# Gate columns moved to the prompt stage, batched state-space tables, and a third PSUM bank for turned weights in an NSA + S5 hybrid decoder step

## The reference

```
proj = einsum('ntd,de->nte', h, w_in)                      # h: normalised, modulated rows
o_cmp = attention over compressed keys (one per 16 tokens, window 32)
o_slc = attention over the 16 best blocks of 64 keys
o_win = attention over the last 512 keys
g_nsa = sigmoid(g_nsa)                                      # one gate for each branch, head and token
o     = g_nsa[0]*o_cmp + g_nsa[1]*o_slc + g_nsa[2]*o_win
# S5: h_t = a*h_{t-1} + B u_t (complex, 32 groups of 64 states, 16 inputs), y = Re(C h) + d*u
o_ssm = gelu(y) * sigmoid(gelu(y) @ w_glu)
x = x + mod2 * ((sigmoid(g_a)*(o @ w_br_attn) + sigmoid(g_s)*(o_ssm @ w_br_ssm)) @ w_out)
y = rms_norm(x + mod5 * (relu(norm(x) @ w_ff1)**2 @ w_ff2), g_final)
```

## Time and profile before

| what | value |
|---|---|
| three runs | 2451.07, 2453.78, 2454.67 us, median 2453.78 |
| the profiled execution | 2447.4 us, its span 2445.6 us |
| mean granted TensorE clock | 0.927 of full speed |
| busy share of the span | PE 88%, DVE 37%, ACT 29%, POOL 21% |
| prompt attention, 768 to 1099 us | PE busy 285.8 of 331 us, ACT 200.6, DVE 188.6 |
| decode attention, 1099 to 1274 us | PE busy 99.0 of 175 us |

### The profile page before, as it was taken

One profiled execution on the slowest core, in us unless ns is written; L12 is line 12 of the kernel. 1 busy time (PEld: TensorE's weight loads), 2 busy tenths in 40 slices (PEclk: granted clock), 3 DMA queues, 4 the chain that ended last, 5 costly groups with the idle time before them and its releaser, 6 DMA issues. The chain is left out here.

```text
span 2445.6 us, 32920 instructions
## 1 busy us (share of the span) xinstructions
PE 2157.7 (88%) x13512; PEld 1812.2 (74%) x13512; DVE 895.2 (37%) x1752; ACT 715.2 (29%) x1485; POOL 514.3 (21%) x506
## 2 busy tenths in 40 slices
PE   7694969978998898884659999999999999999998
PEld 4453645546554566652449999999999999999997
DVE  2597001105442665642453111345412422422424
ACT  3320300003222576652233222333312311311313
POOL 0250000011112654421112211211121122211120
PEclk8886679989998899996879999999999999999999
DMA  8102042325431321106643111311111111111112
GB/s 319 16 1 75 37 114 38 113 73 185 172 138 39 91 74 52 50 26 228 254 182 97 44 51 45 115 35 44 44 48 48 44 44 44 45 51 44 44 54 78
DMA packets 212870, 201.48 MB, mean 82 GB/s; under 512 B 37327, under 2 KB 194999, under 8 KB 204065
## 3 DMA queue, kind: packets, MB, share of 16 engines
q1 hardware_dynamic: 200926, 131.40, 18.3%
q0 software_dynamic: 9216, 67.11, 7.3%
q10 hardware_dynamic: 2578, 0.88, 0.1%
HBM read 177.62 MB, written 21.58 MB: 81 GB/s over the span
## 5 line engine op out<-in xcount | busy, mean ns | idle before, releaser
L2116 PE MATMUL ps<-tail,tail 128*128 128x356 f32 (+2 forms) x2304 | 756.7, 328 | 9.5 <-POOL tail L2514 9.5
L2118 PE MATMUL ps<-tail,tail 128*128 128x356 f32 (+2 forms) x2304 | 750.7, 326 | 0.0
L2117 PE MATMUL ps<-tail,tail 128*128 128x356 f32 (+2 forms) x2304 | 748.9, 325 | 0.0
L2116 PEld LDWEIGHTS ps<-tail,tail 128*128 128x128 f32 x2304 | 435.5, 189 | 12.1 <-POOL tail L2514 9.7
L2117 PEld LDWEIGHTS ps<-tail,tail 128*128 128x128 f32 x2304 | 435.7, 189 | 2.5
L2118 PEld LDWEIGHTS ps<-tail,tail 128*128 128x128 f32 x2304 | 435.8, 189 | 0.0
L2514 POOL TENSOR_TENSOR tail<-tail,tail 128x1024 fp32r<-128x1024 f32 x96 | 232.4, 2421 | 936.9 <-ACT tail L2361 936.9
L2545 DVE SCALAR_TENSOR_TENSOR tail<-ps,mod,tail 128x346 f32<-128x346 f32 (+2 forms) x120 | 68.7, 573 | 344.3 <-PE ps L2118 334.9
L2361 ACT ACTIVATE tail<-tail 128x1024 fp32r<-128x1024 f32 x96 | 101.0, 1053 | 320.2 <-PE ps L2118 314.3
L1609 POOL TENSOR_SCALAR pr<-pr,row_reciprocals,gT 128x640 f32<-128x640 f32 (+7 forms) x128 | 98.7, 781 | 151.4 <-DVE row_reciprocals L1728 150.5
L1256 PE MATMUL ps<-xT,w1T 128*128 128x512 f32 (+1 forms) x288 | 121.7, 579 | 0.0
(11 more groups left out here) (441 smaller groups left out, 2711.6 us busy)
## 6 DMA issues: line engine op xcount, KB each, us to landing
tail<-in_w_ff SPq DMA_DIRECT2D x64, 512.0 KB, 3.8
wada_late<-in_w_ada SPq DMA_DIRECT2D x32, 512.0 KB, 4.2
wada<-in_w_ada SPq DMA_DIRECT2D x4, 2048.0 KB, 11.9
tail<-in_w_in SPq DMA_DIRECT2D x16, 512.0 KB, 3.7
x_keep<-xT SPq DMA_DIRECT2D x1, 4224.0 KB, 11.5
h_keep<-hT SPq DMA_DIRECT2D x1, 4224.0 KB, 13.4
tail<-x_keep SPq DMA_DIRECT2D x1, 4224.0 KB
xrow<-in_x_prompt SPq DMA_DIRECT2D x8, 512.0 KB, 7.2
```

Of the source, the lines that this page charges most:

```text
L2116: pe.matmul(out, whi[:, kw, :], xlo(kx), start=(i == 0), stop=False)
L2117: pe.matmul(out, wlo[:, kw, :], xhi(kx), start=False, stop=False)
L2118: mm = pe.matmul(out, whi[:, kw, :], xhi(kx), start=False, stop=(i == n - 1))
```

## The change

It does five things. The parameters are turned after product group 0 instead of 1, and ScalarE's exponentials and sine move one group earlier with them. The G and F tables are made four powers at a time: each family keeps its six formulas, on 128x1024 elements (the ninth l alone on 128x256), so 102 instructions become 30. In the prompt stage the rotation for turned weights has three banks, 4, 5 and 7, and all blocks accumulate in bank 6; the compressed branch's value product moves from v = 1 to v = 5 and waits for the store of the previous block. The gates of the decode tokens are written to DRAM and read back during the prompt stage, between the loads of the modulation weights: written after load 8, read three columns at a time after loads 12 to 19. `gd` becomes `e.gd`, which lives through both stages. In the decode stage these 25 DMAs and VectorE's wait are gone.

```diff
-                if i == 1:
+                if i == 0:
                     turn_parameters()
...
-                if i == 1:
+                if i == 0:
                     act.wait_ge(S["dt_spread"], 1)
                     act.activation(dtb[:, :], bank[1][:, 0:SG], ACT.Exp).then_inc(S["exp_done"], 1)
-                if i == 2:
+                if i == 1:
                     act.wait_ge(S["magnitudes_ready"], 1)
...
-            for k in range(LC):
-                q = LC + 1 + k
-                link(tt(Gre[:, :, k, :], BBre[:, :, :], tG(pr, q, SI), ALU.mult))
...
+            for k in range(0, LC, 4):
+                ks, q = slice(k, k + 4), LC + 1 + k
+                gr, gi, tg = Gre[:, :, ks, :], Gim[:, :, ks, :], half_of(4)
+                br4, bi4, pr4, pi4 = over_k(BBre[:, :, :], 4), over_k(BBim[:, :, :], 4), powers(pr, q, 4), powers(pi, q, 4)
+                link(tt(gr, br4, pr4, ALU.mult))
+                link(tt(tg, bi4, pi4, ALU.mult))
+                link(tt(gr, gr, tg, ALU.subtract))
...
-            for l in range(LC + 1):
...
+            for l, m in ((0, 4), (4, 4), (8, 1)):
...
-        chunks.setdefault(qb * PER + 1, []).append((qb, None, CMP, 0, 1))
+        chunks.setdefault(qb * PER + 5, []).append((qb, None, CMP, 0, 1))
...
-        outp = lambda qb: bank[6 + qb % 2]
+        outp = lambda qb: bank[6]
+        turn_bank = lambda x: bank[(4, 5, 7)[x % 3]]
...
+                if j == 2 * R:
+                    sp.dma_start(gscr, e.gates[:, T:NT]).then_inc(gates_stored, 16)
+                if 3 * R <= j < 3 * R + NSEQ:
+                    load_wait(sp, gates_stored, 1)
+                    n = j - 3 * R
+                    for br in range(3):
+                        sp.dma_start(e.gd[32 * (n % 4):32 * (n % 4) + 32, n // 4, br:br + 1],
+                                     bass.AP(tensor=gscr.tensor, offset=br * HQ * NS + n * TS, ap=[[NS, HQ], [1, TS]]),
+                                     allow_slow_non_contiguous=True).then_inc(gates_landed, 16)
+            load_wait(sp, gates_landed, 3 * NSEQ)
...
-                if x >= 2:
-                    pe.wait_ge(turned_kept, x - 1)
-                return bank[4 + x % 2]
+                if x >= 3:
+                    pe.wait_ge(turned_kept, x - 2)
+                return turn_bank(x)
...
-                    if qb >= 2:
-                        pe.wait_ge(outputs_kept, qb - 1)
+                    if qb:
+                        pe.wait_ge(outputs_kept, qb)
...
-            sp.dma_start(gscr, e.gates[:, T:NT]).then_inc(gates_stored, 16)
-            load_wait(sp, gates_stored, 1)
-            for n in range(NSEQ):
-                for br in range(3):
-                    sp.dma_start(gd[32 * (n % M):32 * (n % M) + 32, n // M, br:br + 1],
...
-                if b == 0:
-                    load_wait(dve, gates_landed, 3 * NSEQ)
                 dve.tensor_scalar(Sc[:, :], Sc[:, :], gd[:, b, 0:1], None, ALU.mult).then_inc(weights_scaled, 1)
```

47 lines of the change are left out of this document (23 added, 24 removed).

## The result

The changed kernel takes 2386.82 us (median of 4 runs, 2381.71 to 2391.31) against 2452.57 (4 runs, 2451.07 to 2454.67): ratio 0.9731, 95% interval 0.9706 to 0.9755, 65.7 us less. The profiled execution took 2383.85 us, its span 2382.0.

A forecast was written before the change was run, and what follows sets the result against it. It took TensorE's idle time, within stages cut at barriers, as what to explain. Terms -14.0 (gate columns), -25.5 (third bank) and -3.4 (state space) sum to -42.9 us, 2410.9 on the median's basis; predicted 2410, range 2401 to 2426.

The forecast's parts named there:

- Third bank: Prompt stage: a third bank for turned weights removes TensorE's bank waits; term -25.5 us, bounds -11.2 and -28.
- Blocks 0 to 3 ... 0: Prompt stage: blocks 0 to 3 have at most four tiles per unit, so no such bank waits; gain 0.
- the single result bank: Prompt stage: compressed product waits for the previous block's store, up to 0.5 us in seven blocks; 1 us charged.
- the thin margin: Prompt stage: ScalarE's exponential ends only 0.4 us before TensorE needs it; 1.5 us charged for waits that come back.
- Gate columns: Decode stage: removing the gate write, 24 reads and VectorE's wait gives -14.0 us, bounds -11.4 and -15.5.
- The prompt side: Prompt stage: 25 more SP issues for the gates cost 0; upper bound 17 us, not believed.
- State space: State-space stage: earlier, wider table making lets the scan start when the chunk inputs end; -3.4 us, bounds 0 and -4.
- either of the two edits alone would give the same 3.4: State-space stage: early parameter turning or four-power tables, each alone, brings the scan's whole 3.4 us gain.
- ScalarE's pace: Rival, prompt stage: ScalarE, not TensorE, sets the pace; term -11.2 us, time 2425, chance 0.14.
- waits on GpSimd in blocks 4 to 7: Rival, prompt stage: waits come back whole, for weights GpSimd has yet to scale; term 0, time 2436 us, chance 0.04.
- the result bank: Rival, prompt stage: TensorE stands at the compressed product until ScalarE's store, seven times; time 2463 us, chance 0.02.
- Keys made later by the window values: Rival, decode stage: window values compete with gathers, keys 2.5 us later; -10.2 instead of -14, time 2415 us, chance 0.08.

The follow-up runs named there:

- strict_late: Changed kernel with three banks, but every `ada` and `mod` entry waits for ScalarE's copy of the entry right before it; 2454.42 us, ratio 1.0024.
- two_banks: Changed kernel with the third bank alone taken back, banks 4 and 5 for turned weights; 2427.59 us, ratio 0.9907.
- c_undone: Changed kernel with the three PSUM edits taken back: two turned-weight banks, two result banks, compressed product at v = 1; 2425.82 us, ratio 0.9911.
- d_undone: Changed kernel with gates written and read back in the decode stage again, and VectorE's wait there; 2402.53 us, ratio 0.9808.
- after_again: The changed kernel itself, measured once more; 2384.77 us, ratio 0.9736.
- ab_undone: Changed kernel with both state-space edits taken back; 2383.91 us, ratio 0.9741, and 2398.26 us in a second series; ten runs have median 2391.8.
- early_only: Changed kernel with tables G and F again made one power at a time, parameters still turned after group 0; 2388.42 us, ratio 0.975.
- warm_both: Changed kernel plus unread matmuls: 21 ahead of the products of y, three ahead of the turning of U; 2374.90 us, ratio 0.9711.

## Why the prediction was wrong in size

**Third bank: the step that failed.** "The 25.9 us of blocks 4 to 7, and some 2 more ... make 28": that TensorE alone sets the pace was right (pairs of 4.37 us, 168.1 us busy of 169.9), and so was that each wait is worth its full length; but the prediction took the idle column for that length, and it isn't. Whole blocks 4 to 7 hold 30.1 us of idle rows by line where I had 28, and each of 34 waits costs 0.20 us more that stands under busy time, 6.8 us (0.16 to 0.19 in the blocks of strict_late and two_banks whose clock was 1.00). The term as measured is 36.6 us, of which two_banks gives 34.5 to the third bank and 2.1 to the two other edits.

**"Blocks 0 to 3 ... 0"** was wrong too: they fell from 113.6 to 109.8 us. `ada` and `mod` entries take banks there as well (strict_late adds 26 us in them), and before, five waits for a bank in blocks 1 to 3 took 2.2 us, now one takes 0.6. But the largest part, 2.0 us, is in block 0, where nothing waited for a bank: 25.4 us before, 25.5 in c_undone, 23.6 in two_banks and 23.4 now, so it comes with the other two edits (TensorE's waits for weights that GpSimd scales are 3.0 us there in c_undone, 1.2 in two_banks; why isn't shown). Block 1 can't be divided up: with three banks it takes 26.0 to 28.7 us in different profiles, at mean clocks of 0.70 to 0.84.

The charges of 1 us for the single result bank and 1.5 for the thin margin fell due nowhere: L1550 waits 0.1 us in blocks 4 to 7 and 0.3 in block 3, and two_banks makes that pair of edits a gain of 2.1. The first scores of the stage came 1.6 us later, 12.7 us after its start instead of 11.1. That is clock: TensorE is busy throughout with the same 28 rows, at a mean of 0.73 instead of 0.85, and over all profiles it is 11.1 to 11.4 us at 0.81 to 0.85 and 12.6 to 12.7 at 0.73 or 0.74. The sum: 36.6 + 3.7 - 1.6 = 38.7 where 25.5 stood; 28 was set as the far bound, and that bound was an idle time, so the range could not hold the result.

**Gate columns.** -14.0 forecast with -15.5 as the far bound, -15.9 in the first profiles, 17.8 by the medians of d_undone and after_again (15.6 by their profiled spans). The chain from the keys on gained 14.9 instead of 14.3. The rest isn't taken apart: the keys come 19.6 to 27.1 us into the stage whatever the edit, and the mean clock of the stage was 0.75 before and is 0.81 now. The prompt side cost 0, as priced.

**State space.** The -3.4 to the start of the scan is there in every profile with an edit and without extra matmuls ahead of it (40.5 to 40.6 us from L551 against 43.8 to 43.9), and "either of the two edits alone would give the same 3.4" in two. The wide tables cost GpSimd 17.5 us more than the narrow ones (66.9 against 49.4), with 24 instructions of 1.23 us, 29.5 together; the forecast had 29.5 as the most, counted from a chain beside narrow tables. Those hold it up as well (0.38 us for a short instruction instead of 0.22), so the 17.5 are a difference and not the whole of what the wide ones cost. The Trainium skill (SBUF — State Buffer, "Who interferes with whom") says that the one that comes second blocks fully. The trace agrees: beside wide tables even a 16-element instruction of GpSimd takes 1.18 us, about one table instruction. It costs nothing, since the chunk inputs are later still. What the forecast lacked is the 7.1 us of the products of y, a change of clock in them that it put at nothing. Whether the edits have a part in it is open: without the extra matmuls the products took 36.7 us in all three profiles without the edits, and 22.0 to 31.2 in the eleven with one or both. Had the edits no part and every profile the same odds, that split would come up once in 364 times (3! 11! / 14!); yet four runs of ab_undone, of which no profile exists, were as fast as the changed kernel.

**The rivals.** ScalarE's pace, waits on GpSimd in blocks 4 to 7 and the result bank are refuted by the first profile, where TensorE has 0.35 us of idle rows left in these blocks. Keys made later by the window values are not seen either: they came after 24.0 us instead of 25.9, and later than before in only three of the sixteen profiles. (That rival's -10.2 lay outside the term's own bound of -11.4, a slip in the prediction.)

## What to carry to other kernels

Where an engine that is the bound waits many times, compare the length of the whole stretch with and without, or the start-to-start time of a piece with and without its wait: TensorE's idle column leaves out a piece at every wait (0.16 to 0.20 us here, whatever its length), and 34 short waits make that a fifth of the whole (6.8 of 36.6 us). List every user of a rotation before calling a stretch free of its waits; here the two entries that come every few steps carried nearly all the waits, and a bank of their own cured them nearly as well as a third bank for all (2.4 us less). A long wait of TensorE ahead of a long stretch of its work can cost twice: behind 20 us of idle time the products of y took 22.0 to 36.7 us, behind matmuls whose results nothing reads 20.5 to 22.0. Compare profiles by clock before explaining a difference of a few us: block 7 of c_undone, the first scores and the products of y were nothing else.

## What the runs showed of the hardware that I had not expected

- The granted clock of the same products of y, behind the same 20 us of idle time, stayed at 0.50 for all of 36.7 us in three profiles and rose within them in eleven (near 236 us in strict_late, near 241 in early_only, near 255 after the change). The runs of one kernel spread by 3 us (warm_both) to 26 (before, 17 runs), mostly more than the state-space term.
- It fell to 0.50 within a stretch in which TensorE was never idle (near 155 us in warm_both), where the matmuls had 128 and 8 columns.
- Loads beside gathers: the last of four window-key loads of 256 KB was turned 19.6 to 27.1 us after the start of the stage, where their 1.05 MB would take 2.5 at the 421 GB/s of the earlier trace rows; the issues of the next three took 18.94 us together on SyncE's queue.

```profile
1054.31 18.94 SPq L1812 DMA_DIRECT2D vwin<-in_cache_v_win  x3
```
